# A fused two-block transformer kernel: 45 products on zeros between the first eight modulation units, and a buffer that GpSimd clears for them

## The reference

```
cond = silu(c)
for l in range(2):                       # first block
    mod = cond @ w_mod[l] + b_mod[l]     # 1024 x 9216; shift, scale and gate, three times
    sh1, sc1, g1, sh2, sc2, g2, sh3, sc3, g3 = split(mod, 9)
    h = rms_norm(x, norm_g[l, 0]) * (1 + sc1) + sh1
    x = x + 0.5 * g1 * swiglu(h, w_ffn1_gu[l], w_ffn1_down[l])      # 1024 -> 2 x 2816 -> 1024
    h = rms_norm(x, norm_g[l, 1]) * (1 + sc2) + sh2
    x = x + g2 * (mix(three attentions of h) @ w_out[l])
    h = rms_norm(x, norm_g[l, 2]) * (1 + sc3) + sh3
    x = x + 0.5 * g3 * swiglu(h, w_ffn2_gu[l], w_ffn2_down[l])
for l in range(2):                       # second block: retention and pooling, then a swiglu
    ...
return rms_norm(x, final_norm)
```

## Time and profile before

| | us |
|---|---|
| median of the runs | 1761.82 |
| span of the profiled execution | 1759.8 |
| what lies around the span (median less span) | 2.0 |
| TensorE busy | 1732.4 (98%) |
| VectorE, ScalarE, GpSimd busy | 1419.2, 1006.7, 184.0 |
| chain that ended last | TensorE 94%, VectorE 2%, DMA 2% |
| first unit starts | 8.48 |
| unit 15 starts | 29.35 |
| first product of the first strip | 32.59 |

### The profile page before, as it was taken

One profiled execution on the slowest core, in us unless ns is written; L12 is line 12 of the kernel. 1 busy time (PEld: TensorE's weight loads), 2 busy tenths in 40 slices (PEclk: granted clock), 3 DMA queues, 4 the chain that ended last, 5 costly groups with the idle time before them and its releaser, 6 DMA issues.

```text
span 1759.8 us, 24720 instructions
## 1 busy us (share of the span) xinstructions
PE 1732.4 (98%) x9178; PEld 1470.0 (84%) x9178; DVE 1419.2 (81%) x2185; ACT 1006.7 (57%) x1666; POOL 184.0 (10%) x382
## 2 busy tenths in 40 slices
PE   6999999999999999999999999999999999999998
PEld 3888888888888888988888888888888888888886
DVE  7899987898899888878888866579888876688565
ACT  5445577755475556877545644556455544465454
POOL 3021012111111111021110000001110000010000
PEclk9999999999999999999999999999999999999999
DMA  9999742699869985418898654459886483466551
GB/s 352 356 360 393 273 147 83 259 332 337 315 225 340 332 314 205 168 51 317 329 334 291 224 206 158 161 191 333 324 325 249 169 301 146 185 229 245 204 194 70
DMA packets 125144, 441.10 MB, mean 251 GB/s; under 512 B 15248, under 2 KB 18272, under 8 KB 124896
## 3 DMA queue, kind: packets, MB, share of 16 engines
q1 hardware_dynamic: 91024, 316.17, 49.1%
q0 software_dynamic: 33296, 120.12, 18.2%
q10 hardware_dynamic: 704, 3.23, 0.5%
HBM read 438.38 MB, written 1.09 MB: 250 GB/s over the span
## 4 chain that ended last, share of the span: by engine, by line
PE 94%; DVE 2%; DMA 2%; ACT 1%; issue 1%; SPq 0%; DVEq 0%; ACTq 0%
PE banks L2368 24%; PE banks L2169 15%; PE banks L2373 12%; PE banks L2147 11%; PE banks L2174 7%; PE banks L2152 6%; PE banks L2317 2%; PE banks L2321 2%; PE banks L2326 2%; PE banks L2137 1%; PE banks L2139 1%; PE banks L2138 1%; DMA weights_raw<-in_w_mod_first 1%; PE banks L2281 1%; DVE weights_lo L1355 1%
## 5 line engine op out<-in xcount | busy, mean ns | idle before, releaser
L1355 DVE TENSOR_TENSOR weights_lo<-weights_raw,weights_hi 128x1024 fp32r<-128x1024 f32 (+2 forms) x584 | 685.9, 1200 | 67.5 <-ACT weights_hi L810 66.7
L810 ACT ACTIVATE weights_hi<-weights_raw 128x1024 fp32r<-128x1024 f32 (+2 forms) x584 | 584.8, 1036 | 68.3 <-PE banks L2174 21.9
L2368 PE MATMUL banks<-hT,weights_hi 128*128 128x512 f32 x1856 | 464.1, 392 | 0.0
L2368 PEld LDWEIGHTS banks<-hT,weights_hi 128*128 128x128 f32 x1856 | 337.3, 189 | 63.0
L2373 PEld LDWEIGHTS banks<-hT,weights_lo 128*128 128x128 f32 x1856 | 253.2, 190 | 18.1
L1368 DVE CUSTOM_DVE_ANT_0 arena<-arena,mod_acc,vectors 128x1024 f32<-128x1024 f32 x216 | 267.6, 1280 | 0.0
L2373 PE MATMUL banks<-hT,weights_lo 128*128 128x256 f32 x1856 | 258.8, 282 | 0.0
L1004 ACT ACTIVATE arena<-banks 128x512 f32<-128x512 f32 x116 | 69.3, 598 | 323.1 <-PE banks L2373 322.9
L2147 PE MATMUL banks<-weights_hi,hT 128*128 128x512 f32 (+2 forms) x896 | 218.2, 385 | 0.0
L2147 PEld LDWEIGHTS banks<-weights_hi,hT 128*128 128x128 f32 x896 | 165.6, 188 | 29.9
L1690 DVE TENSOR_TENSOR arena<-banks,arena 128x512 f32<-128x512 f32 x116 | 79.8, 688 | 108.9 <-ACT arena L1004 108.9
(11 more groups left out here) (358 smaller groups left out, 1971.3 us busy)
## 6 DMA issues: line engine op xcount, KB each, us to landing
weights_raw<-in_w_ffn_gu SPq DMA_DIRECT2D x176, 512.0 KB, 4.5
arena<-in_w_mod POOLq DMA_DIRECT2D x128, 512.0 KB, 6.2
weights_raw<-in_w_in SPq DMA_DIRECT2D x104, 512.0 KB, 4.1
weights_raw<-in_w_ffn_down SPq DMA_DIRECT2D x88, 512.0 KB, 5.0
arena<-in_w_ada POOLq DMA_DIRECT2D x88, 512.0 KB, 5.6
weights_raw<-in_w_ffn_in SPq DMA_DIRECT2D x88, 512.0 KB, 4.1
weights_raw<-in_w_ffn_out SPq DMA_DIRECT2D x44, 512.0 KB, 4.5
weights_raw<-in_w_out SPq DMA_DIRECT2D x32, 512.0 KB, 3.8
```

The source lines that it names most:

```text
L810: nc.scalar.activation(whi[:, n % PARTS, 0:width], raw[:, slot, 0:width], ACT.Copy).then_inc(S("hi_done"), credit(n))
L1355: V.tensor_tensor(wlo[:, n % PARTS, 0:width], raw[:, n % RING, 0:width], whi[:, n % PARTS, 0:width].bitcast(F32), ALU.subtract).then_inc(S ...
L2368: T.matmul(half_banks(j)[:, kind, :], whi[:, n % PARTS, 256 * k + P * kind:256 * k + P * (kind + 1)], hx[:, :, 4 * q + k, :], start=q == 0 ...
```

## The change

GpSimd writes zeros into all of `hT` as the first of its steps, ahead of the angles; this is one more step in `pool_step`. TensorE waits for `pool_step` 1 before modulation unit 0. Behind each of the units 0 to 7 stands a call of `fillers(u)`, with three rounds of one or two products each that read the zeros and write bank 0 or 1, whose contents nobody reads; 45 products in fifteen forms. All but three have 512 columns. The forms differ in how the moving operand is read (side by side; steps of 2, 4 and 8 elements; turned, with an inner step of 32 or of 2; 16 columns repeated 32 times), in the stationary operand (side by side, a step of 2, one column repeated), in the type (the one-pass float, bf16, plain float32 with 256 columns) and in the number of rows (64 instead of 128).

```diff
+            then(G.memset(hx[:, :, :, :].bitcast(F32), 0.0))
             angles()
             pool.wait_ge(S("hi_done"), RING + PREFETCH)
...
+            def fillers(u):
+
+                z = hx[:, :, :, :].rearrange("p a k n -> p (a k n)")
+                wide = z.bitcast(BF16)
+                for i in range(3):
+                    o = bank[i % 2][:, :]
+                    if u == 0:
+                        T.matmul(o, z[:, 0:P], z[:, 0:512], start=True, stop=True)
+                        T.matmul(o, z[:, 0:P], z[:, 2048:2560], start=True, stop=True)
+                    elif u == 1:
+                        T.matmul(o, z[:, 0:P], z[:, 0:1024:2], start=True, stop=True)
+                    elif u == 2:
+                        T.matmul(o, z[:, 0:P], z[:, 0:2048:4], start=True, stop=True)
+                        T.matmul(o, z[:, 0:P], z[:, 0:4096:8], start=True, stop=True)
+                    elif u == 3:
+                        T.matmul(o, z[:, 0:P], z[:, 0:512].rearrange("p (a b) -> p b a", a=16), start=True, stop=True)
+                        T.matmul(o, z[:, 0:P], z[:, 0:512].rearrange("p (a b) -> p b a", a=256), start=True, stop=True)
+                    elif u == 4:
+                        T.matmul(o, z[:, 0:P], z[:, 8:520], start=True, stop=True)
+                        T.matmul(o, z[:, 0:P], z[:, 0:16].unsqueeze(1).broadcast_to([P, 32, 16]), start=True, stop=True)
+                    elif u == 5:
+                        T.matmul(o, z[:, 0:2 * P:2], z[:, 512:1024], start=True, stop=True)
+                        T.matmul(o, z[:, 0:1].broadcast_to([P, P]), z[:, 512:1024], start=True, stop=True)
+                    elif u == 6:
+                        T.matmul(o, wide[:, 0:P], wide[:, 0:512], start=True, stop=True)
+                        T.matmul(o, wide[:, 0:2 * P:2], wide[:, 0:1024:2], start=True, stop=True)
+                    else:
+                        T.matmul(o[:, 0:256], z.bitcast(F32)[:, 0:P], z.bitcast(F32)[:, 512:768], start=True, stop=True)
+                        T.matmul(o, z[0:64, 0:P], z[0:64, 512:1024], start=True, stop=True)
...
                     pe.wait_ge(S("cond_ready"), 1)
+                    pe.wait_ge(S("pool_step"), 1)
                     for u in range(MOD_FIRST_UNITS):
                         mod_unit(u)
+                        if u < 8:
+                            fillers(u)
```

## The result

| | before | changed |
|---|---|---|
| median of the runs, us | 1761.94 (4 runs) | 1773.51 (4 runs) |
| ratio, 95% interval | 1 | 1.0067 (1.0052 to 1.0081) |
| span of the profiled execution | 1759.8 | 1771.4 |
| unit 0 starts | 8.48 | 8.36 |
| unit 8 starts | 20.07 | 31.98 |

The direction was right and the size was not: 1767.4 with a range of 1765.0 to 1771.3 had been forecast. Unit 8 is 11.9 us late instead of 6.9, and the end is 11.6 us late instead of 5.6.

What follows compares the result with a forecast made beforehand. TensorE was taken to bound the kernel after the opening. Profiled span 1759.8 plus a first-strip delay of 5.6 (6.1 - 0.5) gave 1765.4; with 2.0 to the median, 1767.4 us, range 1765.0 to 1771.3.

Steps and rivals of the forecast that it cites:

- TensorE is the bound and a late opening is passed on: From the first strip to the end: the opening's delay, 5.6 us, is passed on because TensorE is the bound.
- The clearing costs nothing at 0.8 to 1 ns an element: GpSimd's clear before unit 0: ends at 3.7 to 4.5 us, before the pairs land, and costs nothing.
- That makes 42 + 6 = 48 counts: Products behind units 0 to 7: 45 products priced as 48 counts of 0.226 us, making unit 8 6.9 us later.
- both bounds of the forecast: TensorE's opening: clock comes up at 12.0 or 15.4 us, putting unit 8 at 26.0 or 27.6; 27.0 taken.
- Rival C: Units 1 to 3 and 6: stepped operands cost double, nine products 2.0 us (1769.4) or eighteen 4.1 (1771.5); chance 0.25.
- So TensorE, and no longer the DMA stream, ends the opening: Units 14 and 15: tile 15 lands at 34.2, before unit 15 at 35.4, so no wait; unit 15 +6.1 us.
- the 1.3 us that were taken off for it: Unit 8 to first strip: delay falls from 6.9 to 6.1 at unit 15, then by 0.5 at ScalarE, to 5.6.
- The 4.5: DMA of tile 15: once the backlog has run dry, a tile lands 4.5 us after its issue.
- the 0.8 of the forecast: Units 14 and 15: without waits for tiles, the delay falls from unit 8's 6.9 us to +6.1 at unit 15.
- The 0.5 behind it: Before the first strip: ScalarE's first tile comes ahead of its modulation step, winning back 0 to 0.8 us, 0.5 taken.
- The backlog lets unit 8 be some 3 us late: Tile stream in the opening: tile 14 waited 7.3 us from issue against 4.5 without a queue, leaving some 3 us.
- rival A: Opening: TensorE's waits and the backlog hide the products if under about 0.1 us each; 1761.8 us; chance 0.06.

Runs made afterwards that it cites:

- e2: Flat kernel: changed kernel with all 45 products as 128x512 one-pass float, side by side, at the same places; 1768.88 us, ratio 1.0039.
- e3: Changed kernel with only the 15 products behind units 1, 2 and 3 reading side by side instead of with steps; 1770.59 us, ratio 1.0052.
- e4: Changed kernel with only the six products behind unit 7 made 128x512 side by side; 1772.27 us, ratio 1.0061.
- e8: Changed kernel with two rounds instead of three, 30 products, all 128x512 side by side; 1765.54 us, ratio 1.0022.
- e1: Changed kernel with the clear and the wait kept and all 45 products left out; 1761.82 us, ratio 0.9999.
- e5: Changed kernel with tiles 14 and 15 landing in two buffers of their own, issued without waiting for units 8 and 9; 1772.17 us, ratio 1.0055.
- e12: Changed kernel with unit 7's six products grouped, three plain float32 then three on 64 rows, instead of in turn; 1773.25 us, ratio 1.0065.
- e9: Changed kernel with 16 instead of 8 keep-warm products on zeros ahead of the first strip; 1774.28 us, ratio 1.0068.
- e7: Changed kernel with one round instead of three, 15 products, all 128x512 side by side; 1762.60 us, ratio 1.0002.
- e10: Changed kernel with eight products of one form behind each of units 0 to 7; one run, read for pitches: bf16 step 8 took 0.90 us each.

## Why the forecast was wrong, point by point

- "TensorE is the bound and a late opening is passed on": right. Unit 8's delay and the end's are 11.9 and 11.6 us in the profiles, and in e2, e3, e4 and e8 the end moved with unit 8 (7.8 and 6.9; 9.1 and 8.6; 10.9 and 10.2; 4.5 and 3.9 us).
- "The clearing costs nothing at 0.8 to 1 ns an element": right, 0.86 ns; e1 shows no cost.
- **The step that failed: "That makes 42 + 6 = 48 counts" of 0.226 us.** The sum took the price of a product side by side, without a change of rows, for all fifteen forms. The 15 products with steps took 1.55 us behind unit 1, 2.75 behind unit 2 and 2.85 behind unit 3, where the flat kernel takes 0.89, 1.50 and 1.58: 3.2 us more. The three pairs behind unit 7 took 3.16 instead of 1.59: 1.6 more. The rest is in the flat ones: each group of products costs some 0.1 us at its start, and a unit between them 0.57 instead of 0.49; e2's unit 8 is at 27.9 against the forecast's 27.0, with 45 counts and not 48. Sum: 0.9 + 3.2 + 1.6 = 5.7 against 5.0 found (31.98 - 27.0). Of the remaining 0.7, 0.6 is the clock, which in the changed kernel came up at some 11.5 us, ahead of both bounds of the forecast (12.0 and 15.4): the products behind unit 1 start at 12.44 there and at 13.00 in e2. That is luck of this execution. The bf16 products behind unit 6 are the other 0.1 or so.
- Rival C had the right kind. It doubled nine products for 2.0 us, or eighteen with the bf16 ones for 4.1. Fifteen were doubled, for 3.2 us: step 2 as well, bf16 with step 2 not. Its times, 1769.4 and 1771.5, are below 1773.51 because they stand on the same sum of flat prices, with neither the changes of rows nor the wait for tile 15. The Trainium skill, page "SBUF — State Buffer", section "Door 1: The DMA port swizzle", lets accesses pass at full pace that hit a line of 16 bytes at least twice, and makes a crossing to a new line pay. The traces agree that long steps cost, and not with the free ones: step 2 in 4-byte floats has two hits in a line and costs 0.48. The measurement decides.
- The change between 128 and 64 rows was in no rival. It costs 0.19 us each time, and 1.1 us in the six behind unit 7.
- **"So TensorE, and no longer the DMA stream, ends the opening" and the 1.3 us that were taken off for it (6.9 to 5.6): wrong.** Tile 15 was issued behind unit 9, with the first feed-forward tiles right behind it, and landed 6.3 us after its issue, not 4.5. The 4.5 was the median over a whole kernel's feed-forward tiles. In the kernel before the same load took 6.4 us, so the backlog that had gone shortened tile 14's (7.2 to 3.7) and not tile 15's. Unit 15 waited 0.63 us, and ScalarE's rounding still stood directly ahead of its modulation step at 43.31, as before at 31.56. e5 shows the size: 1.3 us. The landing of tile 15 differs between executions, 5.4 us in e12, 5.6 in e2, 7.0 in e9. In e2 the tile did arrive in time for unit 15 (35.79), and the row behind unit 15 starts 7.0 us late (36.91 against 29.92) at unit 8's 7.8: the 0.8 of the forecast is found. The 0.5 behind it is not: the first strip stands 7.2 us late (39.81), since ScalarE's tile came at 37.82, directly ahead of its modulation step at 38.78.
- "The backlog lets unit 8 be some 3 us late" was given as a condition of rival A, and it is too much. Unit 8 is 1.1 us late in e7 at no cost that can be measured; from there to e8 it moves by 3.4 us and the time by 2.9. With 3 us free, e8's 4.5 us would have cost 1.5; they cost 3.9 (interval 2.3 to 5.3).
- The forecast's own range, 1765.5 to 1769.0, is wider than the bounds that it names: unit 8 at 26.0 with 0.8 won back gives 1766.1, at 27.6 with nothing won back 1768.5. Both stay under the result.

## What to carry to other kernels

A product's price is that of its operands' form, so a pitch read from products side by side is no price for one with steps. In these runs it doubles for 4-byte floats with steps of 2 to 32 and for bf16 with a step of 4, and is four times as much for bf16 with a step of 8; for any other form, time eight in a row. Work put ahead of a stage that streams from memory is free only as far as the engine would have waited there: 15 products went into the waits, and nearly all the time of the next 30 was found at the end of the kernel, though the engine had been idle for a quarter of that stretch. Buffers that are given back late were the smaller part, 1.3 of 11.6 us. Products on 64 rows belong together, not in turn with those on 128.

## What the runs showed of the hardware that was not expected

- A product whose moving operand is 4-byte one-pass floats costs 0.44 to 0.48 us for 512 columns with steps of 2, 3, 4, 8 or 32 elements alike, twice the 0.23 of side by side; one in bf16 costs 0.22 with steps of 1 and 2, 0.46 with 4, 0.90 with 8. Reading from two places 256 elements apart in turn is as fast as side by side (0.24). For bf16 this fits a price per line of 16 bytes; the 4-byte floats, which stop at double, do not follow it, and that is left open.
- The stationary operand with a step of 2, or one column repeated, costs nothing: 0.23 between the rows of unit 5.
- The clock fell in the middle of dense rows. In e10 the eight bf16 products with step 8 started with a granted clock of 1.00, and they follow each other without a wait from 27.59 to 34.78; the clock stood at 0.50 (1.2 GHz) from 32 to 34 us. The steps behind them ran at that level too: the bias pass took 1.14 us and unit 5 1.08, where 0.69 and 0.64 are usual at full clock. Behind unit 5 it came up again. TensorE was busy 2.00 of 2.00 us throughout. The eight stand 0.90 us apart at either level (28.47, 29.38, 30.28, 31.18, 32.08 and 32.98).
- A product on 64 rows costs about what one on 128 does (0.255 and 0.23), but each change between them 0.19 us.
